# Depthwise causal convolution on TensorE: diagonal taps and VectorE taps replaced by four shifted copies of 32 channels and four column strips

## What is computed

```python
def conformer_conv(g, dw_w, dw_b, ln_g, ln_b):
    u = g[..., :CONV_CHANNELS] * jax.nn.sigmoid(g[..., CONV_CHANNELS:])
    y = lax.conv_general_dilated(
        u, dw_w[:, None, :].astype(u.dtype), window_strides=(1,),
        padding=[(CONV_WIDTH - 1, 0)], dimension_numbers=('NWC', 'WIO', 'NWC'),
        feature_group_count=CONV_CHANNELS) + dw_b
    return jax.nn.silu(layernorm(y, ln_g, ln_b))

def even_mixer(t, layer_idx, w_in, lq1, lk1, lq2, lk2, subln, dw_w, dw_b, ln_g, ln_b, w_out, cos, sin):
    proj = t @ w_in
    y_a = diff_attention(proj[..., :3 * DIFF_WIDTH], layer_idx, lq1, lk1, lq2, lk2, subln, cos, sin)
    y_b = conformer_conv(proj[..., 3 * DIFF_WIDTH:], dw_w, dw_b, ln_g, ln_b)
    return jnp.concatenate([y_a, y_b], axis=-1) @ w_out
```

## Time and profile before

| | |
|---|---|
| median of 3 runs | 1879.71 us |
| the profiled execution, its own time | 1879.24 us |
| its span in the profile | 1877.4 us |
| TensorE busy | 1818.6 us of the span |
| VectorE busy | 771.5 us |
| ScalarE busy | 940.2 us |
| GpSimd busy | 1373.7 us |
| mean granted TensorE clock | 0.994 of 2.4 GHz |

### The profile page before, as it was taken

The page is one execution under the profiler, slowest core; times in us unless marked ns, Lnnn a source line. Parts: engine busy times, 40 slices in busy tenths (PEclk is TensorE's granted clock), DMA queues, the critical chain, the costliest instruction groups (busy, mean ns, idle before and its releaser), DMA issues.

```text
span 1877.4 us, 27931 instructions
## 1 busy us (share of the span) xinstructions
PE 1818.6 (97%) x9322; PEld 1452.8 (77%) x9322; DVE 771.5 (41%) x1494; ACT 940.2 (50%) x1481; POOL 1373.7 (73%) x803
## 2 busy tenths in 40 slices
PE   8999999998999999999999999999999999999997
PEld 6677888765788887677888877778888877778886
DVE  2493533374355564453111555451113745451112
ACT  5556444444644464555444545654445555654443
POOL 5437999526798869668888884578887884578884
PEclk9999999999999999999999999999999999999999
DMA  8737666578887745445666453356654553356652
GB/s 281 240 124 231 192 189 201 192 232 295 269 277 244 252 142 183 135 124 171 213 198 190 148 169 99 102 157 200 208 186 157 162 175 101 101 158 190 190 185 72
DMA packets 251081, 344.24 MB, mean 183 GB/s; under 512 B 20464, under 2 KB 150640, under 8 KB 250992
## 3 DMA queue, kind: packets, MB, share of 16 engines
q1 hardware_dynamic: 248848, 337.06, 56.2%
q10 hardware_dynamic: 2144, 6.03, 1.0%
HBM read 341.96 MB, written 1.05 MB: 183 GB/s over the span
## 4 chain that ended last, share of the span: by engine, by line
PE 85%; DVE 8%; ACT 2%; issue 1%; POOL 1%; DMA 1%; SPq 1%; DVEq 0%; ACTq 0%; POOLq 0%
PE bank L2309 24%; PE bank L2311 24%; PE bank L2310 24%; PE bank L2395 3%; PE bank L2956 2%; PE bank L2983 2%; PE bank L2966 2%; DVE arena L1730 1%; PE bank L2361 1%; DMA raw<-in_l_w_in 1%; PE bank L2419 0%; ACT wh L782 0%; DVE X L1469 0%; ACT xf L866 0%; PE bank L2450 0%
## 5 line engine op out<-in xcount | busy, mean ns | idle before, releaser
L755 POOL TENSOR_TENSOR wl<-raw,wh 128x1024 fp32r<-128x1024 f32 x300 | 733.4, 2456 | 110.0 <-ACT wh L947 84.1
L2309 PE MATMUL bank<-wh,xh 128*128 128x512 f32 (+2 forms) x1726 | 681.0, 395 | 10.5 <-POOL wl L719 2.4
L2311 PE MATMUL bank<-wl,xh 128*128 128x512 f32 (+2 forms) x1726 | 665.4, 386 | 0.0
L2310 PE MATMUL bank<-wh,xl 128*128 128x512 f32 (+2 forms) x1726 | 664.7, 385 | 0.0
L722 POOL TENSOR_TENSOR wl<-raw,wh 128x512 fp32r<-128x512 f32 (+2 forms) x234 | 319.0, 1363 | 326.5 <-ACT wh L782 326.5
L947 ACT ACTIVATE wh<-raw 128x1024 fp32r<-128x1024 f32 x270 | 286.2, 1062 | 436.2 <-PE bank L2311 422.2
L2309 PEld LDWEIGHTS bank<-wh,xh 128*128 128x128 f32 x1726 | 325.2, 188 | 85.5 <-issue 13.6
L2311 PEld LDWEIGHTS bank<-wl,xh 128*128 128x128 f32 x1726 | 324.8, 188 | 66.0
L2310 PEld LDWEIGHTS bank<-wh,xl 128*128 128x128 f32 x1726 | 325.6, 189 | 60.1
L782 ACT ACTIVATE wh<-raw 128x1024 fp32r<-128x1024 f32 (+2 forms) x268 | 275.8, 1050 | 163.7 <-PE bank L2311 99.5
L723 POOL TENSOR_TENSOR wl<-raw,wh 128x512 fp32r<-128x512 f32 (+2 forms) x234 | 308.3, 1318 | 0.0
(11 more groups left out here) (372 smaller groups left out, 1748.0 us busy)
## 6 DMA issues: line engine op xcount, KB each, us to landing
raw<-in_w_ffn_in SPq DMA_DIRECT2D x264, 256.0 KB, 3.0
raw<-in_w_in SPq DMA_DIRECT2D x224, 256.0 KB, 2.9
raw<-in_w_mod SPq DMA_DIRECT2D x152, 256.0 KB, 4.0
raw<-in_w_ffn_out SPq DMA_DIRECT2D x132, 256.0 KB, 2.9
raw<-in_l_w_gate SPq DMA_DIRECT2D x88, 256.0 KB, 3.9
raw<-in_l_w_up SPq DMA_DIRECT2D x88, 256.0 KB, 4.7
raw<-in_l_w_down SPq DMA_DIRECT2D x88, 256.0 KB, 3.6
raw<-in_l_w_in SPq DMA_DIRECT2D x48, 256.0 KB, 4.6
```

What stands on the lines that cost most here:

```text
L755: nc.gpsimd.tensor_tensor(wl[:, s, :], raw[:, s, :], words(wh)[:, s, :], ALU.subtract)\
L2309: mm(dst, x_hi, w_hi, start=first, stop=False, skip_group_check=True)
L2310: mm(dst, x_lo, w_hi, start=False, stop=False, skip_group_check=True)
L2311: return mm(dst, x_hi, w_lo, start=False, stop=last, skip_group_check=True)
```

## The change

The convolution is computed on TensorE alone. For each block of 32 channels (strip q of tile c) a copy `shifted` holds the same 32 channels four times, 32 rows each, copy j shifted by j tokens; it is made by four transfers from `uT` in SBUF to `shifted` in SBUF. A stationary of 128 x 32, `tap_w`, holds four taps of these 32 channels as four stacked diagonals, so one matmul adds four taps of 32 channels. Eight matmuls (`TAP_GROUPS`) with the moving operand starting 4 columns further each time give 32 taps (the 32nd weight is zero). Four strips of a tile go to four 32-column strips of the array, next to each other in the program: 4 tiles x 8 groups x 4 strips = 128 matmuls.

`shifted` covers two tiles at once (b = 0 for tiles 0 and 1, b = 1 for tiles 2 and 3), so there are 8 copies and 32 transfers, each 32 partitions x 2 x 284 float32 (73 KB). ScalarE issues 20 of them right behind the second `evac_u` and ahead of the `Exp` of `log_dt` and of the rounding for tile 4 of `in0`, and 12 behind the last `evac_qk0`. VectorE builds `tap_w` at the start with one reduction and four multiplies of 128 x 1024. The 62 diagonals on ScalarE and the 62 multiply-adds on VectorE go.

```diff
-        tap_ring = view("l0", 16, P)
+        tap_w = arena[:, 0:CONV_T * 4 * TAP_GROUPS * 32].rearrange("p (n c) -> p n c", c=32)
+        shifted = [view("l0", 2, TAP_COLS) for _ in range(5)]
+        shifted += [Y.rearrange("p t d -> p (t d)")[:, 2 * TAP_COLS * i:2 * TAP_COLS * i + 2 * TAP_COLS]
+                    .rearrange("p (a b) -> p a b", a=2) for i in range(3)]
...
# ScalarE
-            in0_until(2, 0)
-            taps(0, 8)
...
+            def shift_copies(b, strips):
+
+                for q in strips:
+                    for j in range(4):
+                        act.dma_start(shifted[4 * b + q][32 * j:32 * j + 32], uT[32 * q:32 * q + 32, 2 * b:2 * b + 2, j:j + TAP_COLS])\
+                           .then_inc(shift_in[b], 16)
             in0_until(2, 3)
             evac_u(0)
-            taps(8, 16)
             in0_until(3, 1)
             evac_u(1)
+            act.wait_ge(u_ev, 2)
+            shift_copies(0, range(4))
+            shift_copies(1, range(1))
             nc.scalar.activation(dt, V_("log_dt"), ACT.Exp).then_inc(disc_a, 1)
...
             evac_qk0(2)
             evac_qk0(3)
-            taps(16, 22)
+            shift_copies(1, range(1, 4))
+
+            def evac_conv(b):
+                act.wait_ge(tap_used, b + 1)
+                for c in range(2 * b, 2 * b + 2):
+                    nc.scalar.activation(yc[:, c, :], scratch[:, SEQ * (c % 2):SEQ * (c % 2) + SEQ], ACT.Identity, bias=V_("dw_b", c))\
+                      .then_inc(tap_out, 1)
...
+            evac_conv(0)
             act.wait_ge(wt_tr, 1)
...
-            taps(22, 44)
...
-            taps(44, PE_TAPS)
...
-            act.wait_ge(tap_used, PE_TAPS)
-            for c in range(2):
...
+            evac_conv(1)
             hi_until(plan.first["out0"] + 4)
# VectorE
             v.tensor_copy(cw[:, :, 22:24], csilu.rearrange("p (k s) -> p k s", s=2)).then_inc(c_set, 1)
 
+            dve.wait_ge(ident_in, 16)
+            step(v.tensor_reduce(tap_mask[:, :], ident.rearrange("p (j c) -> p c j", c=32), AX_X, ALU.add))
+            settle()
+            w = V_("dw_w").unsqueeze(2)
+            for c in range(CONV_T):
+                n = slice(4 * TAP_GROUPS * c, 4 * TAP_GROUPS * c + 4 * TAP_GROUPS)
+                v.tensor_tensor(tap_w[:, n], spread(tap_mask[:, :].unsqueeze(1), 4 * TAP_GROUPS, 32),
+                                spread(w[:, n], 4 * TAP_GROUPS, 32), ALU.mult).then_inc(tap_set, 1)
...
-            dve.wait_ge(u_ev, 1)
-            dve.wait_ge(lo_ready, plan.split(plan.end("in0")))
-            conv(14)
...
-            conv(26)
...
-            conv(4)
...
-            conv(2 * CONV_W - conv_at[0])
-            settle()
-            v.engine_nop().then_inc(conv_y, 1)
# TensorE
+            def conv(b, first, last, mods):
+
+                j0, pieces, n = plan.first[mods], plan.end(mods) - plan.first[mods], last - first
+                for i in range(first, last):
+                    for j in range((i - first) * pieces // n, (i + 1 - first) * pieces // n):
                         mod_chunk(j0 + j)
+                    e, g = divmod(i, TAP_GROUPS)
+                    for q in range(4):
+                        ins = mm(scratch[32 * q:32 * q + 32, SEQ * e:SEQ * e + SEQ], tap_w[:, (4 * (2 * b + e) + q) * TAP_GROUPS + g, :],
+                                 shifted[4 * b + q][:, e, 4 * g:4 * g + SEQ], start=g == 0, stop=g == TAP_GROUPS - 1,
+                                 skip_group_check=True)
+                if last == 2 * TAP_GROUPS:
                     ins.then_inc(tap_used, 1)
 
+            pe.wait_ge(tap_set, CONV_T)
             pe.wait_ge(u_ev, 2)
-            conv(0, 12, "mod0_scores")
+            pe.wait_ge(shift_in[0], 16 * 16)
+            conv(0, 0, 2 * TAP_GROUPS, "mod0_scores")
             pe.wait_ge(w_done, 1)
...
-            conv(12, 24, "mod0_rows")
+            pe.wait_ge(shift_in[1], 16 * 16)
+            pe.wait_ge(tap_out, 2)
+            conv(1, 0, 6, "mod0_rows")
...
-            conv(24, 36, "mod0_turned")
+            conv(1, 6, 10, "mod0_turned")
...
-            conv(36, PE_TAPS, "mod0_values")
+            conv(1, 10, 2 * TAP_GROUPS, "mod0_values")
...
-            pe.wait_ge(conv_y, 1)
-            pe.wait_ge(tap_out, 2)
+            pe.wait_ge(tap_out, CONV_T)
```

More of the change, by code:

```diff
@@ L317, in build @@
         hot = sb("hot", [P, 56])
+        tap_mask = sb("tap_mask", [P, 32])
         raw = sb("raw", [P, RING, HALF])
@@ L992, in in0_until @@
                 hi_until(plan.tiles["in0"][i][2][part][0] + RING)
[L994 to L1000, removed]
             in0_until(1, 3)
@@ L1716, in _ @@
             take_rotated(3, DW, back)
-            conv_at = [0]
-            def conv(n):
-                for _ in range(n):
-                    w, c = divmod(conv_at[0], 2)
-                    conv_at[0] += 1
-                    tap = V_("dw_w", c * CONV_W + w)
-                    if w == 0:
-                        step(v.tensor_scalar(yc[:, c, :], uT[:, c, 0:SEQ], tap, V_("dw_b", c), ALU.mult, ALU.add))
-                    else:
-                        settle(1)
-                        ins = v.scalar_tensor_tensor(out=yc[:, c, :], in0=uT[:, c, w:w + SEQ], scalar=tap, in1=yc[:, c, :],
-                                                     op0=ALU.mult, op1=ALU.add)
-                        step(ins)
             def weights(qb):
@@ L2627, in _ @@
                 ins.then_inc(sc_done, 1)
-            def conv(first, last, mods):
-                j0, pieces = plan.first[mods], plan.end(mods) - plan.first[mods]
-                for n in range(first, last):
-                    for j in range((n - first) * pieces // (last - first), (n + 1 - first) * pieces // (last - first)):
+            def conv(b, first, last, mods):
+                j0, pieces, n = plan.first[mods], plan.end(mods) - plan.first[mods], last - first
+                for i in range(first, last):
+                    for j in range((i - first) * pieces // n, (i + 1 - first) * pieces // n):
                         mod_chunk(j0 + j)
-                    w, c = divmod(n, 2)
-                    pe.wait_ge(tap_set, n + 1)
-                    ins = mm(scratch[:, SEQ * c:SEQ * c + SEQ], diagonal[n % 32], uT[:, 2 + c, w:w + SEQ], start=n == 0,
-                             stop=w == CONV_W - 1, skip_group_check=True)
+                    e, g = divmod(i, TAP_GROUPS)
[4 more added lines that the diff above has]
+                if last == 2 * TAP_GROUPS:
                     ins.then_inc(tap_used, 1)
+            pe.wait_ge(tap_set, CONV_T)
             pe.wait_ge(u_ev, 2)
-            conv(0, 12, "mod0_scores")
+            pe.wait_ge(shift_in[0], 16 * 16)
+            conv(0, 0, 2 * TAP_GROUPS, "mod0_scores")
             pe.wait_ge(w_done, 1)
```

22 lines of the change are left out of this document (11 added, 11 removed).

## The result

The changed kernel takes 1887.8 us (median; 1884.3 to 1892.0) against 1879.7 for the kernel before (1877.5 to 1881.3) on the same chip: ratio 1.0043, 95% interval 1.0035 to 1.0051. It is slower by 8 us, where 1875.4 was forecast, in a range that ended at 1886. The profiled execution of after took 1889.55 us, with a span of 1887.7.

The account below looks back on a forecast made before the run. TensorE, busy 97% of the span, was taken as the bound. From the scores on -16.0, then +7.5 issues, +1.5 clock, +2.7 `tap_w` gave -4.3 us: 1875.4 us against the median, range 1867 to 1886.

Parts of the forecast that it names:

- The taps (-13.5): Convolution on TensorE: 32 fours of strips at 0.43 us, 13.8 us, replace 62 taps taking 27.3: 13.5 us less.
- the modulation chunks (-0.8): Modulation chunks inside a convolution piece now match their neighbours' shape: six save 0.14 us each, 0.8 us less.
- the wait for VectorE (-4.3): End of the convolution: TensorE's wait for VectorE's last taps goes with those taps, 4.3 us less.
- Two waits inside the convolution (+3.3): TensorE waits 1.2 us for tiles 0 and 1 behind the exponentials and 2.1 for the attention norm: 3.3 us more.
- The 20 issues (+7.5): Ahead of tile 4 of `in0`: 20 issues of 0.43 us on ScalarE, 8.6, less 1.1 in hand: TensorE loses 7.5 us.
- The rival for slower: ScalarE's queue fills and issues cost more: gain gone from 0.56 us each, slower by 0.2% from 0.68; chance 0.17.
- The clock (+1.5 and +0.8): Low TensorE clock: 1.5 us lost after the idle time at tile 4, 0.8 after the two convolution waits.
- Building `tap_w` (+2.7): At the start, VectorE's four multiplies alternate with GpSimd's low halves, so TensorE loses 2.7 us.
- The other reading, GpSimd shut out: At the start, GpSimd waits for all four multiplies: 3.9 us instead of 2.7; as rival with clock falls, 1878.8, chance 0.22.
- The freed diagonals (0.2 at most): In `in0`, ScalarE is free earlier without the diagonals: worth 0.2 us at most, counted as nothing.
- The data in time: The transfers' 2.3 MB cross while the ring's loads stand still; the second twelve have 7 us until wanted; no loss.
- The rival in which the issues don't hold ScalarE: Issue time lies beside ScalarE's other work, so tile 4 and the exponentials aren't late: -14.5 us, 1865; chance 0.12.

Follow-up runs that it names:

- the late build: Changed kernel with `tap_w` built where VectorE's first 14 old taps stood, after GpSimd's last low half for `in0`, instead of at the start: 1884.0 us, ratio 1.002.

## Why the prediction was wrong, step by step

- **The taps (-13.5), the modulation chunks (-0.8), the wait for VectorE (-4.3): right.** A four costs 0.43 (6.69 us for 15 of them). Without transfers the mean starts 115.61 - 85.68 = 29.9 us behind the scores; 29.3 was forecast, 45.0 was before. All in all -16.4 against -16.0; the modulation chunks' 0.8 was not measured by itself. That the total fits so well is in part luck: the -16.0 holds 1.2 of wait for the twelve issues and 0.8 of clock, and the kernel without transfers has 0.37 and 1.7 in their place.
- **Two waits inside the convolution (+3.3): half right.** The wait for the attention norm was put at 2.1 and is 1.98 in nearly every kernel. The one behind the exponentials was put at 1.2, from 12 issues of 0.43. Twelve took 8.9 us (102.15 to 111.07) instead of 5.2, so that even the softmax weights were late: 3.43 + 0.70.
- **The 20 issues (+7.5): the step that failed.** "I stay at 0.43 because it is the same queue, back to back." The row was a pair that loads from HBM. From SBUF to SBUF an issue takes 0.61 to 0.62 on the same queue, 0.69 with the gaps and the one long one in twenty: 13.9 us instead of 8.6, and with 1.0 in hand instead of 1.1 a stop of 12.96 instead of 7.5. The queue was not what mattered: SyncE pays 0.60 for the same transfers and 0.43 for most of its loads from HBM. The upper bound, 0.64, was nearer by luck: its four issues are loads from HBM too, of 0.49 to 0.79 us, where the 52 of that group have a median of 0.432. The rival for slower named this mechanism and its threshold (0.68 an issue for 0.2%), with 0.17. It came true, though not by a queue that fills: the price is the same for a whole block (median 0.618, shortest 0.600).
- **The clock (+1.5 and +0.8): mis-sized.** One stop, one fall of 1.5 us was taken from rows 3. After 12.96 us of idleness 1.2 GHz stayed for 6.2 us of work, 3.1 us lost. Inside the convolution it stayed from 116.8 to 123.6, about 3.1, and again behind the 1.98 us wait, 1.7. Of 15.8 us ahead of the scores, 12.96 + 3.1 = 16.1 is the account; of the 6.7 behind, 4.13 less the 0.37 that is there without transfers, 3.8, and 3.1 for the clock, 6.9, is the account. The step on the issues alone would have stayed in the range: 5.5 us more in front of tile 4 and 4.13 - 1.2 = 2.9 in the convolution make 1883.8. The clock's 1.6 and 2.3 us beyond the forecast make it 1887.7.
- **Building `tap_w` (+2.7): right**, at 2.2 to 3.4 in the traces and 3.8 and 1.9 in the two comparisons of runs, and the engines take turns. The other reading, GpSimd shut out, did not happen with multiplies of two tensors. Why the 5.33 us of rows 6 was so long was not tried.
- **The freed diagonals (0.2 at most): about right.** From the third chunk to the first of tile 4, without its stop, the late build has 66.08 - 26.54 = 39.5 us against 68.33 - 28.52 = 39.8.
- **The data in time: right** in the changed kernel, wrong to be taken as given elsewhere: with all on SyncE's queue it was 3.94 us late. That it crosses while the ring's loads stand still is wrong: loads were in flight and took up to 9.5 us instead of 4.6, which the stop of 12.96 us hid.
- **The rival in which the issues don't hold ScalarE** is out: the table load stood for 13.92 us behind them. It is true only of an instruction ahead of them (70.39 and 70.40). The Trainium skill, "DMA: Bandwidth & Descriptors", section Issuing engines are not separate DMA queues, has the issue time as usually small beside the transfer. For a single transfer the trace agrees in that the issue is the shorter part, 0.62 us against a median of 5.7 from issue to landing for the first twenty and 2.1 for the twelve; but the sentence does not price the block, which held ScalarE for 13.9 us.

The sum with the measured terms: the forecast, 1875.4, had 9.0 for the first twenty and 1.2 + 0.8 for the wait and the clock behind them; the runs showed 15.8 and 6.7, that is 11.5 more, 1886.9. The rest to 1887.8 is in the spread. So the step that failed is the price of an issue, 0.43 where 0.69 was measured in a block, and with it the price of the low clock, 1.5 and 0.8 where 3.1 and 3.1 were lost.

## What to carry to other kernels

A DMA issue is an instruction of its engine's queue: price it by a row whose two ends lie in the same memories, multiply by the count, and ask which computing instruction stands behind the block. Spread issues beside long instructions of the same engine, or give them to a queue in which nothing waits, early enough for the data, and use few large transfers. Then look at what their data does to the loads that cross beside them. When a stop is added, add the work at the lower clock behind it: where the clock fell in these traces, 1.5 to 3.1 us were lost, and the length of the stop does not tell how much (1.8 behind 12.56 us in the kernel with the strips one by one, 3.0 behind 3.98 in the one with 8 transfers, 1.7 behind 1.98).

## What the runs showed that was not expected

- An issue's price follows where the two ends lie: 0.443 us from HBM to SBUF, 0.345 from SBUF to HBM, 0.60 to 0.62 from SBUF to SBUF, for 16 or 32 partitions and one or two pieces, and there 0.64 to 0.69 for 128 partitions.
- Issues and a computing instruction that stands ahead of them run at the same time on ScalarE (70.39 and 70.40); a computing instruction behind them waits for the last.
- Products of one strip of 32 columns take 0.39 us each, four in different strips 0.43 together, and between these two kernels only the order differs.
- The same 1.98 us wait was followed by the low clock in the changed kernel and in the one without transfers, but not with 20 transfers between the roundings and twelve on SyncE, whose first fall behind it came at 173.6 us. What decides that stays open.
